# Supertile 3's norm moved behind up product 11 and turned by DMA, with one final tile on ScalarE and GpSimd

## The chip, the cores and the metric

One Trainium2 chip; the same program runs on 8 cores, each with its own tokens. The time is device microseconds of the slowest core, so it ends when the last of the eight is done. A core has a matmul engine (TensorE, PE in the rows, with PEld for its weight loads), VectorE (DVE), ScalarE (ACT), GpSimd (POOL), a queue for transfers issued by SyncE (SP), and 16 DMA engines that all queues share.

## The reference, cut to what matters

```python
def _layer(x, pool_hist, pos0, norm1_g, w_in, ...):
    h = _rmsnorm(x, norm1_g)
    z = h @ w_in                                   # [pool | u | v], 1536 columns
    a, u, v = z[..., :512], gelu(z[..., 512:1024]), gelu(z[..., 1024:])
    pool_out, new_hist = _pool_mixer(a, pool_hist, pos0, pool_w, pool_scale)
    gmlp_out = _gmlp_gate(u, v, gmlp_ws, gmlp_b)
    x = x + concatenate([pool_out, gmlp_out], axis=-1) @ w_out
    f = _rmsnorm(x, norm2_g) @ w_up                # 1024 -> 4096
    return x + square(relu(f)) @ w_down            # 4096 -> 1024
# one layer, then a final _rmsnorm(x, normf_g) is stored as y
```

## The kernel before

A core has 33 tiles of 128 tokens, in 11 **supertiles** of three tiles (384 tokens), numbered 0 to 10. The residual rows of supertile i stand in buffer `X[i % 3]`, three tiles of 512 KB each. Supertiles 0 and 1 share their MLP (the pair products, lines 667 and 687); from supertile 2 on the loop at line 963 does one at a time, and the front part of supertile i+1 (norm, input projection, mixers, output projection) is laid between the MLP products of supertile i.

The **MLP** of a supertile is 32 up products (`gen_UP`, PE line 705, eight matmuls each, then relu on ScalarE, line 709, and a square on VectorE, line 711), and eight groups of down products (`gen_DN`, line 764). The weights stream from the scratch tensor `scr` through a ring of five 1 MB slots, `RING`. When the last product that reads a slot has been issued, `ring_next` puts the load of the block five places on into SyncE's queue (line 650); it waits there for that product.

The **up products** use five PSUM banks in turn; product m uses bank (m+3) % 5, so product 0 needs bank 3, which the pair down products (line 687, added to X by VectorE at line 691) have used just before.

The **norm** of a supertile (`gen_N1_elem`) is three squares on ScalarE with a running sum (line 317), two small GpSimd instructions (lines 324, 330), and three multiplies on VectorE into the buffers `HB` (line 341). `gen_N1_T` then turns each tile for the input projection into `HT`: for supertiles 0 to 3 by eight transposes on PE (line 352) and a copy on ScalarE (line 356); from supertile 4 on by one DMA transpose from SyncE's queue for each tile (line 362). The input projection `gen_WI_au` (PE line 432) reads all three tiles of `HT`.

The **final norm** (`gen_final`) is three squares, two GpSimd instructions and three VectorE multiplies (line 802); the stores to `yall` are issued by SyncE for supertile 0 (`gen_ystore`, line 813) and by GpSimd for the others. The x loads (`gen_L`, line 268) go through GpSimd's queue, but those of supertile 3 go through SyncE's. A load of x into a buffer waits until the stores that read the buffer have landed.

The order of every engine's work is that of the `add` calls in the program; each engine runs its own list in order, and a wait holds all that stands behind it on the same engine. Around the change the order is: `gen_pair_DN(3, 0, 0)`, `(3, 1, 0)`, the final norm of supertile 0, `gen_pair_DN(3, 0, 1)`, a ring load, the stores of supertile 0, `gen_pair_DN(3, 1, 1)`, a ring load, the final norm of supertile 1 with its stores, the x loads of supertile 3, and then the loop for supertile 2 (line 970 on).

Of the kernel before, what the change touches and what calls it, by code (L numbers as in the profile page):

```python
# [8 lines left out]
AF = mybir.ActivationFunctionType  # L9
ALU = mybir.AluOpType  # L10
# [3 lines left out]
NT = 3  # L14
# [21 lines left out]
class Prog:  # L36
# [12 lines left out]
    def add(self, eng, fn, reads=(), writes=(), dma=None, after=()):  # L49
        waits = [self.lastw[k] for k in after]  # L50
        for r in reads:
            w = self.lastw.get(r)
            if w is not None:
                waits.append(w)
        for wr in writes:
            w = self.lastw.get(wr)
            if w is not None:
                waits.append(w)
            waits.extend(self.readers.get(wr, ()))
        ch = self.engchan[eng] if dma is None else self.chan(dma, 16)  # L60
        ch.count += ch.inc
        ev = Ev(ch, ch.count)
        for r in reads:
            self.readers.setdefault(r, []).append(ev)
        for wr in writes:
            self.lastw[wr] = ev
            self.readers[wr] = []
        self.ops[eng].append((fn, waits, ch))
        return ev
# [48 lines left out]
def build_nc():  # L118
# [28 lines left out]
    with contextlib.ExitStack() as es:  # L147
# [116 lines left out]
        def gen_L(i, q="pool"):  # L264
            b = i % NXB
            for n in range(NT):
                t = i * NT + n
                add(q, lambda e, b=b, n=n, t=t: e.dma_start(out=X[b][:, n, :], in_=xall[t * 128:(t + 1) * 128, :]),
                    writes=[("X", b, n)], dma=f"xld{b}_{n}{q}")
# [143 lines left out]

        def gen_N1_T(i, n0=0, n1=NT):
            for n in range(n0, n1):
                if i > 3:
                    norm_T_dma(hbs[("1", i)][n], HT, ("HT", n), 16 + n * 128, f"tr1_{n}")
                else:
                    B = bufs(i)
                    norm_T(hbs[("1", i)][n], B.HT, B.HTk[n], B.ho + n * 128)  # L420
# [232 lines left out]
        def ring_next(i, q):  # L653
            ring_load(ring_at[(i, q)] + NRING)
# [24 lines left out]
        def gen_pair_DN(b, hh, h):  # L679
            q = 8 + 4 * hh + b  # L680
            s = ring_slot(0, q)
            for n in range(NT):
                ub = next_up()

                def mm(e, n=n, s=s, ub=ub):
                    for kk in range(8):
                        i_ = e.matmul(bank(ub)[:, :], lhsT=ST[:, h * 8 + kk, n * 128:(n + 1) * 128], rhs=RING[s][:, kk, :],  # L687
                                      start=(kk == 0), stop=(kk == 7))
                    return i_
                add("pe", mm, reads=[("ST", h * 8 + kk) for kk in range(8)] + [("RING", s)], writes=[("BANK", ub)])  # L690
                add("dve", lambda e, n=n, ub=ub: e.tensor_tensor(  # L691
                    out=X[h][:, n, hh * 512:(hh + 1) * 512], in0=bank(ub)[:, :], in1=X[h][:, n, hh * 512:(hh + 1) * 512],
                    op=ALU.add),
                    writes=[("BANK", ub), ("X", h, n)])

        def gen_UP(i, m0, m1):
            H2all = [("H2T", n) for n in range(NT)]
            for m in range(m0, m1):
                q = m // 4
                s = ring_slot(i, q)  # L700
                ub = (m + 3) % 5

                def mm(e, m=m, s=s, ub=ub):
                    for k in range(8):
                        i_ = e.matmul(bank(ub)[:, 0:TOK], lhsT=RING[s][:, k, (m % 4) * 128:(m % 4 + 1) * 128],  # L705
                                      rhs=H2T[:, k, :], start=(k == 0), stop=(k == 7))
                    return i_
                add("pe", mm, reads=H2all + [("RING", s)], writes=[("BANK", ub)])
                add("act", lambda e, m=m, ub=ub: e.activation(out=ST[:, m, :], in_=bank(ub)[:, 0:TOK], func=AF.Relu),  # L709
                    writes=[("BANK", ub), ("ST", m)])  # L710
                add("dve", lambda e, m=m: e.tensor_tensor(out=ST[:, m, :], in0=ST[:, m, :], in1=ST[:, m, :], op=ALU.mult),  # L711
                    writes=[("ST", m)])
                if m % 4 == 3:
                    ring_next(i, q)
# [77 lines left out]
                    gen_tail(i, n, 1, 512 + p0, 512 + p1, ub, n + j, j == len(parts) - 1)  # L792
                gen_tail_out(i, n)

        def gen_final(i, tiles=None, squares_done=False, store=True):
            b = i % NXB
            tiles = list(range(NT)) if tiles is None else tiles
            srcs = [(X[b][:, n, :], [("X", b, n)]) for n in tiles]
            norm_stats("f", srcs, squares_done=squares_done)
            for j, n in enumerate(tiles):  # L800
                t = i * NT + n
                add("dve", lambda e, n=n, j=j: e.scalar_tensor_tensor(  # L802
                    out=X[b][:, n, :], in0=X[b][:, n, :], scalar=RS["f"][:, j:j + 1], in1=GFB[:],
                    op0=ALU.mult, op1=ALU.mult),
                    reads=[("RS", "f", j), "GFB"], writes=[("X", b, n)])
            if store:
                gen_ystore(i, tiles)

        def gen_ystore(i, tiles, q="pool"):
            b = i % NXB  # L810
            for n in tiles:
                t = i * NT + n
                fin_y[(q, b, n)] = add(q, lambda e, n=n, t=t: e.dma_start(out=yall[t * 128:(t + 1) * 128, :], in_=X[b][:, n, :]),
                                    reads=[("X", b, n)], dma=f"yst{b}_{n}{q}")
# [137 lines left out]
        gen_N2_T(2)  # L952
        gen_pair_DN(3, 0, 0)
        gen_pair_DN(3, 1, 0)
        gen_final(0, store=False)
        gen_pair_DN(3, 0, 1)
        ring_next(0, 11)
        gen_ystore(0, range(NT), "sp")
        gen_pair_DN(3, 1, 1)
        ring_next(0, 15)  # L960
        gen_final(1)
        gen_L(3, "sp")
        for i in range(2, NS):
            nxt = i + 1 < NS
            last = i == NS - 1
            gen_UP(i, 0, 4)
            if i > 2 and i + 2 < NS:
                gen_L(i + 2)
            if i == 2:
                gen_UP(i, 4, 17)  # L970
                gen_N1_elem(3)
                gen_L(4)
                gen_UP(i, 17, 22)
                for n in range(NT):
                    gen_N1_T(3, n, n + 1)
                    gen_UP(i, 22 + n, 23 + n)
                gen_WI_au(3)
                gen_WI_v(3)
                gen_PL(3)
                gen_UP(i, 25, 27)  # L980
                pieces = gen_PG_pieces(3)
                for k in range(4):
                    pieces[k]()
                    gen_UP(i, 27 + k, 28 + k)
                gen_UP(i, 31, 32)
                gen_WO_pe(3)
                gen_N2_elem(3)
                gen_DN(i, 0, 0)
                gen_DN(i, 0, 1)
                gen_DN(i, 0, 2)  # L990
                gen_N2_T(3)
            else:
                gen_UP(i, 4, 8)
                if nxt:
                    gen_WI_au(i + 1)
                    gen_WI_v(i + 1)
                    gen_PL(i + 1)
                gen_UP(i, 8, 18)
                pieces = gen_PG_pieces(i + 1) if nxt else []
                for k in range(8):  # L1000
                    if pieces and k % 2 == 0:
                        pieces[k // 2]()
                    gen_UP(i, 18 + k, 19 + k)
                gen_UP(i, 26, 30)
                if nxt:
                    gen_WO_pe(i + 1)
                    gen_N2_elem(i + 1)
                gen_UP(i, 30, 32)
                if last:
                    add("act", lambda e: e.activation(out=JUNK[:, 0:4], in_=RT[:], func=AF.Sqrt),  # L1010
                        reads=[("RT", n) for n in range(4)], writes=["JUNK"])
                gen_DN(i, 0, 0)
                gen_DN(i, 0, 1)
                gen_DN(i, 0, 2)
                if nxt:
                    gen_N2_T(i + 1)
            gen_DN(i, 0, 3, tile_final=last)
            if last:
                gen_DN_last(i)
                break  # L1020
            gen_DN(i, 1, 0)
            if i < NS - 2:
                gen_N1_elem(i + 2)
            gen_DN(i, 1, 1)
            gen_DN(i, 1, 2)
            if i + 2 < NS:
                gen_N1_T(i + 2)
            gen_DN(i, 1, 3)
            gen_final(i)
# [69 lines left out]
```

How the kernel before makes its waits and increments, by code:

```python
        def run(engname, e, final=False):  # L77
            waited = {}
            pe_ch = prog.engchan["pe"]
            for fn, waits, chn in prog.ops[engname]:
                need = {}
                for w in waits:
                    if engname == "pe" and w.chan is pe_ch:
                        continue
                    if w.val > need.get(w.chan, 0):
                        need[w.chan] = w.val
                for ch, v in need.items():
                    if waited.get(ch, 0) >= v:
                        continue
                    e.wait_ge(ch.sem, v)
                    waited[ch] = v
                ins = fn(e)
                ins.then_inc(chn.sem, chn.inc)
            if final:
                for ev in final_waits:
                    e.wait_ge(ev.chan.sem, ev.val)
```

## Time and profile before

| | us |
|---|---|
| median of 3 runs | 1247.89 (1247.71 to 1248.1) |
| the profiled execution | 1248.57 |
| span of its slowest core, core 4 | 1247.0 |
| spans of the other cores | 1242.1 to 1245.2 |
| PE busy on core 4 | 1232.1 (99%) |
| DVE, ACT, POOL busy on core 4 | 502.7, 374.6, 97.1 |

The profile is of one execution, on every core. A span is from the first to the last instruction of a core. The chain that ended last follows the last instruction back to what released it, and so on. In a row of a timeline the square bracket is the idle time of the engine before the group, and what ended it. "To landing" is the time from the issue of a transfer to the last of its semaphore updates.

### The profile page before, as it was taken

How to read it: one execution, taken by the hardware profiler on the slowest of the kernel's cores; microseconds unless marked ns; L12 is line 12 of the kernel's file. 1: busy time of each engine (PE TensorE's matmuls, PEld its weight loads, DVE VectorE, ACT ScalarE, POOL GpSimd, SP SyncE). 2: the span in 40 equal slices, each digit the busy share in tenths (PEclk: the TensorE clock that was granted, in tenths of full speed). 3: DMA queues.
4: the chain of work that ended last, by engine and by line, in shares of the span. 5: the costliest groups of instructions: out<-in, count | busy, mean ns of one | idle time of the engine just before them, and what ended most of it. 6: DMA issues, size and time to landing. Idle time of an engine off the chain costs nothing.

```text
span 1247.0 us, 19037 instructions; the slowest of 8 cores (1242.1 to 1247.0 us)
## 1 busy us (share of the span) xinstructions
PE 1232.1 (99%) x6777; PEld 651.3 (52%) x6777; DVE 502.7 (40%) x924; ACT 374.6 (30%) x722; POOL 97.1 (8%) x171
## 2 busy tenths in 40 slices
PE   8999999999999999999999999999999999999998
PEld 4455545545545554554555455455545545554554
DVE  5664434444533442543344254234415433450313
ACT  5353313125322330432233043223304322420422
POOL 5010000001010010100001010100101010000000
PEclk9999999999999999999999999999999999999999
DMA  8999967459449537745853874585378448547862
GB/s 175 176 221 222 242 161 199 112 142 322 157 131 257 203 127 227 240 169 157 257 195 130 225 253 169 152 248 195 135 227 260 169 143 244 156 145 228 253 203 85
DMA packets 90671, 240.48 MB, mean 193 GB/s; under 512 B 57665, under 2 KB 57729, under 8 KB 67794
## 3 DMA queue, kind: packets, MB, share of 16 engines
q1 hardware_dynamic: 78480, 189.74, 49.2%
q0 software_dynamic: 11920, 49.19, 17.0%
q8 instruction: 56, 0.92, 0.3%
q10 hardware_dynamic: 178, 0.33, 0.1%
q14 instruction: 37, 0.30, 0.1%
HBM read 214.40 MB, written 34.43 MB: 200 GB/s over the span
## 4 chain that ended last, share of the span: by engine, by line
PE 96%; DMA 2%; POOL 1%; DVE 0%; issue 0%; ACT 0%; SPq 0%; POOLq 0%; ACTq 0%; DVEq 0%
PE ps L705 30%; PE ps L764 28%; PE ps L589 9%; PE ps L432 8%; PE ps L667 7%; PE ps L687 7%; PE ps L457 5%; PE ps L786 2%; DMA WV<-w_v 1%; PE ps L537 1%; DMA X<-xall 1%; PE ps L352 1%; POOL RS L330 0%; POOL RS L324 0%; DVE HB L341 0%
## 5 line engine op out<-in xcount | busy, mean ns | idle before, releaser
L705 PE MATMUL ps<-H2T,RING 128*128 128x384 bf16 x2304 | 384.1, 327 | 0.5 <-DVE X L691 0.5
L764 PE MATMUL ps<-RING,ST 128*128 128x512 bf16 x1632 | 353.7, 380 | 0.0
L705 PEld LDWEIGHTS ps<-H2T,RING 128*128 128x128 bf16 x2304 | 223.8, 98 | 147.8 <-issue 0.9
L764 PEld LDWEIGHTS ps<-RING,ST 128*128 128x128 bf16 x1632 | 159.6, 98 | 191.8
L317 ACT ACTIVATE JUNK<-X 128x1024 bf16<-128x1024 f32 (+2 forms) x104 | 106.4, 1023 | 436.0 <-DVE X L771 290.1
L709 ACT ACTIVATE ST<-ps 128x384 bf16<-128x384 f32 x288 | 140.5, 489 | 208.5 <-PE ps L705 208.4
L711 DVE TENSOR_TENSOR ST<-ST 128x384 bf16<-128x384 bf16 x288 | 96.9, 357 | 193.7 <-ACT ST L709 193.4
L771 DVE TENSOR_TENSOR X<-ps,X 128x512 f32<-128x512 f32 x48 | 33.2, 692 | 222.3 <-PE ps L764 222.3
L432 PE MATMUL ps<-HT,WAU 128*128 128x384 bf16 (+1 forms) x640 | 106.7, 327 | 1.4 <-DMA WAU<-w_au 1.4
L432 PEld LDWEIGHTS ps<-HT,WAU 128*128 128x128 bf16 x640 | 62.3, 98 | 43.4 <-issue 2.4
L687 PE MATMUL ps<-RING,ST 128*128 128x512 bf16 x384 | 83.7, 379 | 0.1
L593 DVE TENSOR_TENSOR X<-ps,X 128x512 f32<-128x512 f32 x66 | 45.5, 691 | 57.9 <-PE ps L589 57.7
L672 ACT ACTIVATE ST<-ps 128x384 bf16<-128x384 f32 x64 | 31.4, 490 | 105.0 <-PE ps L667 101.1
L589 PE MATMUL ps<-WOUT,DT 128*128 128x512 bf16 x240 | 61.6, 380 | 0.0
L589 PE MATMUL ps<-WOUT,MIXT 128*128 128x512 bf16 x240 | 61.6, 379 | 0.0
L687 PEld LDWEIGHTS ps<-RING,ST 128*128 128x128 bf16 x384 | 37.3, 98 | 45.4 <-issue 0.8
L457 PE MATMUL ps<-WV,HT 128*128 128x512 bf16 x240 | 55.1, 388 | 2.5 <-DMA WV<-w_v 2.5
L691 DVE TENSOR_TENSOR X<-ps,X 128x512 f32<-128x512 f32 x48 | 32.5, 690 | 46.2 <-PE ps L687 46.2
L341 DVE SCALAR_TENSOR_TENSOR HB<-X,RS,G1B 128x1024 bf16<-128x1024 f32 x33 | 41.1, 1282 | 23.8 <-DMA H2T<-HB 11.7
L324 POOL TENSOR_SCALAR RS<-SS 128x3 f32<-128x3 f32 (+2 forms) x28 | 14.8, 527 | 460.6 <-ACT JUNK L317 460.3
L802 DVE SCALAR_TENSOR_TENSOR X<-X,RSf,GFB 128x1024 f32<-128x1024 f32 x30 | 36.8, 1282 | 31.2 <-POOL RSf L330 26.8
L341 DVE SCALAR_TENSOR_TENSOR HB<-X,RS,G2B 128x1024 bf16<-128x1024 f32 x30 | 36.8, 1281 | 23.2 <-POOL RS L330 23.2
(103 smaller groups left out, 732.9 us busy)
## 6 DMA issues: line engine op xcount, KB each, us to landing
RING<-scr SPq DMA_DIRECT2D x144, 1024.0 KB, 5.5
RING<-w_mlp POOLq DMA_DIRECT2D x16, 1024.0 KB, 16.6
scr<-RING SPq DMA_DIRECT2D x16, 1024.0 KB, 10.4
yall<-X POOLq DMA_DIRECT2D x27, 512.0 KB, 11.5
X<-xall POOLq DMA_DIRECT2D x24, 512.0 KB, 5.5
X<-xall SPq DMA_DIRECT2D x9, 512.0 KB, 7.7
yall<-X SPq DMA_DIRECT2D x5, 512.0 KB, 8.2
WOUT<-w_out POOLq DMA_DIRECT2D x2, 1024.0 KB, 26.7
```

What stands on the lines that cost most here:

```text
L317: add("act", lambda e, ap=ap, j=j: e.activation(out=JUNK[0:np_, 0:ap.shape[-1]], in_=ap, func=AF.Square, scale=1.0 / 32, accum_out=SS[kind ...
L341: add("dve", lambda e: e.scalar_tensor_tensor(out=HB[hb][:], in0=ap, scalar=RS[kind][:, j:j + 1], in1=gb[:], op0=ALU.mult, op1=ALU.mult), ...
L432: i_ = e.matmul(bank(fb)[:, h0:16 + TOK], lhsT=WAU[:, m, k, :], rhs=B.HT[:, k, ho - 16 + h0:ho + TOK], start=(k == 0), stop=(k == 7))
L457: i_ = e.matmul(bank(fb)[:, :], lhsT=B.HT[:, k, B.ho + n * 128:B.ho + (n + 1) * 128], rhs=WV[:, k, :], start=(k == 0), stop=(k == 7))
L589: i_ = e.matmul(bank(fb)[:, :], lhsT=src[:, n * 128:(n + 1) * 128], rhs=WOUT[:, hh, k, :], start=(k == 0), stop=(k == 7))
L593: add("dve", lambda e, n=n, hh=hh, fb=fb: e.tensor_tensor(out=X[b][:, n, hh * 512:(hh + 1) * 512], in0=bank(fb)[:, :], in1=X[b][:, n, hh * ...
L667: i_ = e.matmul(bank(ub)[:, 0:TOK], lhsT=RING[s][:, k, (m % 4) * 128:(m % 4 + 1) * 128], rhs=HX[:, k, :], start=(k == 0), stop=(k == 7))
L687: i_ = e.matmul(bank(ub)[:, :], lhsT=ST[:, h * 8 + kk, n * 128:(n + 1) * 128], rhs=RING[s][:, kk, :], start=(kk == 0), stop=(kk == 7))
L705: i_ = e.matmul(bank(ub)[:, 0:TOK], lhsT=RING[s][:, k, (m % 4) * 128:(m % 4 + 1) * 128], rhs=H2T[:, k, :], start=(k == 0), stop=(k == 7))
L709: add("act", lambda e, m=m, ub=ub: e.activation(out=ST[:, m, :], in_=bank(ub)[:, 0:TOK], func=AF.Relu), writes=[("BANK", ub), ("ST", m)])
L711: add("dve", lambda e, m=m: e.tensor_tensor(out=ST[:, m, :], in0=ST[:, m, :], in1=ST[:, m, :], op=ALU.mult), writes=[("ST", m)])
L764: i_ = e.matmul(bank(n)[:, :], lhsT=ST[:, kg * 8 + kk, n * 128:(n + 1) * 128], rhs=RING[s][:, kk, :], start=(kg == 0 and kk == 0), stop=(k ...
```

## The change

Three parts. The norm of supertile 3 and its turning move from behind up product 16 (and 21 to 24) of supertile 2 to behind up product 11; the turning goes by DMA from SyncE's queue instead of PE and ScalarE; the x loads of supertile 4, which stand behind the norm in GpSimd's queue, move along. The stores of supertile 0 and the x loads of supertile 3 each stand one ring load earlier in SyncE's queue. In the final norm of supertile 0, tile 2 is scaled by ScalarE and multiplied by the gain on GpSimd, in place of one VectorE instruction.

```diff
         def gen_N1_T(i, n0=0, n1=NT):
             for n in range(n0, n1):
-                if i > 3:
+                if i > 2:
                     norm_T_dma(hbs[("1", i)][n], HT, ("HT", n), 16 + n * 128, f"tr1_{n}")
...
-        def gen_final(i, tiles=None, squares_done=False, store=True):
+        def gen_final(i, tiles=None, squares_done=False, store=True, apart=()):
...
+                if n in apart:
+                    add("act", lambda e, n=n, j=j: e.activation(out=X[b][:, n, :], in_=X[b][:, n, :], func=AF.Copy,
+                                                                scale=RS["f"][:, j:j + 1]),
+                        reads=[("RS", "f", j)], writes=[("X", b, n)])
+                    add("pool", lambda e, n=n: e.tensor_tensor(out=X[b][:, n, :], in0=X[b][:, n, :], in1=GFB[:], op=ALU.mult),
+                        reads=["GFB"], writes=[("X", b, n)])
+                    continue
...
-        gen_final(0, store=False)
+        gen_final(0, store=False, apart=(2,))
+        gen_ystore(0, range(NT), "sp")
         gen_pair_DN(3, 0, 1)
         ring_next(0, 11)
-        gen_ystore(0, range(NT), "sp")
         gen_pair_DN(3, 1, 1)
+        gen_L(3, "sp")
         ring_next(0, 15)
         gen_final(1)
-        gen_L(3, "sp")
...
-                gen_UP(i, 4, 17)
+                gen_UP(i, 4, 12)
                 gen_N1_elem(3)
+                gen_N1_T(3)
                 gen_L(4)
-                gen_UP(i, 17, 22)
-                for n in range(NT):
-                    gen_N1_T(3, n, n + 1)
-                    gen_UP(i, 22 + n, 23 + n)
+                gen_UP(i, 12, 25)
                 gen_WI_au(3)
```

## Rows read from the trace of the kernel before

**Rows 1.** Page of core 4: busy time of the engines; chain that ended last.

```profile
PE 1232.1 (99%) x6777; PEld 651.3 (52%) x6777; DVE 502.7 (40%) x924; ACT 374.6 (30%) x722; POOL 97.1 (8%) x171
...
PE 96%; DMA 2%; POOL 1%; DVE 0%; issue 0%; ACT 0%; SPq 0%; POOLq 0%; ACTq 0%; DVEq 0%
```

**Rows 2.** Spans and granted clocks of the cores.

```profile
core 1: 1245.1 us, clock 0.999
...
core 4: 1247.0 us, clock 0.999
```

**Rows 3.** Chain that ended last, core 4, 270 to 315 us: start, duration, what.

```profile
277.28 1.29 DVE X L691 x2
...
278.71 26.18 PE ps L705 x160
...
308.11 0.61 PE ps L352 x8
...
310.02 0.45 PE ps L352 x8
...
313.51 1.59 PE ps L432 x9
```

**Rows 4.** Busy windows, core 1, 276 to 318 us: engines, PEclk, DMA share, GB/s.

```profile
276.00:318.00 42.00, 41.04 (x267) 24.64 (x266) 20.13 (x40) 23.45 (x44) 5.57 (x10) 1.00 0.99 314
```

**Rows 5.** Timeline of PE, core 1, 274 to 320 us: start, duration, instruction.

```profile
276.73 26.16 PE L705 MATMUL ps<-H2T,RING 128*128 128x384 bf16 x160 [0.48 <-DVE X L691]
303.23 2.76 PE L705 MATMUL ps<-H2T,RING 128*128 128x384 bf16 x16 [0.34 <-ACT JUNK L317]
...
311.49 8.77 PE L432 MATMUL ps<-HT,WAU 128*128 128x384 bf16 x53
```

**Rows 6.** Timeline of DVE, core 4, 225 to 345 us.

```profile
271.89 3.68 DVE L802 SCALAR_TENSOR_TENSOR X<-X,RSf,GFB 128x1024 f32<-128x1024 f32 x3 [3.16 <-POOL RSf L330]
275.49 3.67 DVE L691 TENSOR_TENSOR X<-ps,X 128x512 f32<-128x512 f32 x6
```

**Rows 7.** Groups by line: POOL of core 4, whole run; ACT line 743.

```profile
L249 POOL TENSOR_SCALAR_AFFINE_SELECT IDB<-IDB 128x128 bf16<-128x128 bf16 x1 | 0.3, 292 | 0.2 <-POOL IDB L248 0.2
...
L743 ACT ACTIVATE X<-X,RSf x3: 722/722/722, 1230.0 to 1243.4; 128x512 f32<-128x512 f32 x3
```

**Rows 8.** Core 4: SP timeline, DMA issues at 385 and 391.5 us, line 362.

```profile
385.69 0.32 SPq L650 DMA_DIRECT2D RING<-scr  x1
386.16 6.58 SPq L362 DMA_TRANSPOSE HT<-HB  x3
...
391.51 1.23 SPq L362 DMA_TRANSPOSE HT<-HB  x1
...
RING<-scr SPq DMA_DIRECT2D x1, 1024.0 KB, 5.8
...
HT<-HB SPq DMA_TRANSPOSE x1, 4.5
...
DMA to landing us min/median/max: 3.1/5.8/7.9
```

**Rows 9.** DMA issues of core 1, 285.5 to 286.2 us, then 292 to 293 us: to landing.

```profile
yall<-X POOLq DMA_DIRECT2D x1, 512.0 KB, 14.3
...
RING<-scr SPq DMA_DIRECT2D x1, 1024.0 KB, 16.6
```

**Rows 10.** Timeline of POOL, core 1, 270 to 320 us.

```profile
285.84 0.53 POOL L813 DMA_DIRECT2D yall<-X  x1 [0.65 <-DVE ST L711]
...
303.63 0.89 POOL L330 TENSOR_TENSOR RS<-RS,NEGH 128x3 f32<-128x3 f32 x1
304.49 1.68 POOL L268 DMA_DIRECT2D X<-xall  x3
```

**Rows 11.** DMA packets: core 1, 271 to 312 us; core 4, 273 to 310.9 us.

```profile
DMA packets 2256, 11.47 MB, mean 280 GB/s; under 512 B 238, under 2 KB 238, under 8 KB 1478
...
DMA packets 2236, 11.64 MB, mean 307 GB/s; under 512 B 240, under 2 KB 240, under 8 KB 1394
```

**Rows 12.** DMA by queue, core 4, 312 to 316 us: packets, MB, share.

```profile
q0 software_dynamic: 243, 0.91, 74.5%
q1 hardware_dynamic: 45, 0.24, 24.0%
```

**Rows 13.** PE timelines 40 to 53 us of cores 4, 1; core 4's busy windows.

```profile
44.94 7.03 PE L457 MATMUL ps<-WV,HT 128*128 128x512 bf16 x24 [2.51 <-DMA WV<-w_v]
...
44.43 5.34 PE L457 MATMUL ps<-WV,HT 128*128 128x512 bf16 x24 [1.73 <-DMA WV<-w_v]
...
45.00:50.00 5.00, 5.00 (x16) 1.90 (x17) 1.65 (x6) 0.60 (x1) 1.78 (x3) 0.66 1.02 170
```

## The prediction

> **What bounds the kernel now.** I read the page first: PE is busy for 99% of the slowest core's span, and 96% of the chain that ended last lies on it [rows 1]. So a microsecond counts only where PE stands still or does work that the change removes, and almost all that the change touches on other engines is worth nothing by itself. Then the spans: core 4 sets the time at 1247.0 us, but core 1 is only 1.9 us behind, at 1245.1 [rows 2], so a wait that hits core 1 harder than core 4 can make core 1 the last. The chain around the change [rows 3] shows what there is to win. PE waits for two VectorE evictions before up product 0 starts at 278.71, then 20 up products run in 26.18 us (1.31 each), then come two more, the first transposes at 308.11, and the input projection of supertile 3 at 313.51. Last I read the DMA, because the change turns a PE step into transfers: on core 1, from 276 to 318 us, the engines' share is 0.99 at 314 GB/s [rows 4]. The DMA is as full there as PE is. A transfer that is moved there does not run beside others, it runs behind or between them.
>
> **Part 1, PE loses the transposes.** On core 4, 22 products of 1.30 us end at 278.71 + 28.6 = 307.31. The three products between the transposes take 3.90. The projection starts at 313.51, so 313.51 - 307.31 - 3.90 = 2.30 us are transposes (0.61 for the first group, 0.45 for one later) and the wait ahead of them [rows 3]. Without them the projection could start 32.5 us (25 products) behind product 0. ScalarE also loses three copies, which cost the path nothing.
>
> **Part 2, the wait of product 0.** PE stands 0.48 us before product 0, on core 1 too [rows 5]. On VectorE the three final multiplies start at 271.89 and the six evictions behind them at 275.49 [rows 6]. With two multiplies the evictions begin 1.2 us sooner; the one that product 0 needs is then no longer late, and next to come is the last pair product itself. I take 0.48 us. The new GpSimd multiply has no row of its kind. From below: the VectorE one takes 1.28 us (3.68 for three, overlapped). From above: GpSimd's select of 128 columns took 0.29 us [rows 7], an estimate of 2.3 us for 1024 columns if all of it scales. ScalarE's scaling of 512 columns took 0.72 us [rows 7], so about 1.1 for 1024, in time in which ScalarE has nothing to do. Tile 2 would then be stored from about 275 or 276 us on, as before (its store was issued as the third, behind 271.89 + 3.68 = 275.57). Nobody but that store and what stands behind it waits for GpSimd.
> The page "SBUF — State Buffer" of the Trainium skill (section "Who interferes with whom") says that a VectorE instruction with two SBUF inputs and a GpSimd one that reads SBUF do not run together, and the second to issue waits for the whole of the first. No row here has such a pair of that length. It speaks against this part; what it would do is rival 3.
>
> **Part 3, SyncE's queue.** The stores of supertile 0 go ahead of one ring load, the x loads of supertile 3 ahead of another. The ring load that is now behind the x loads is needed by up product 16, 20.8 us behind product 0; all of it is the same bytes in another order, and I cost it at nothing. Its cover is thin on core 1, where PE already waited 0.34 us before product 20 at 303.23 [rows 5], hidden until now by the wait for the transposes; up to 1 us more if that cover goes. The bounds are 0 and 1.
>
> **Part 4, the turning by DMA.** This is where I expect the result. The norm is five products earlier (6.5 us, plus the 0.48), so `HB` is ready about 22 us behind product 0, and SyncE can issue the three transposes from there. The projection wants them landed at 32.5. How long they take: in a later supertile a ring load was issued at 385.69 and landed 5.8 us later, at 391.5. The three transposes were issued from 386.16, but the third not until 391.51, that is when the ring load had landed, and it landed 4.5 us after that; the shortest of all 48 took 3.1 [rows 8]. So transposes don't overtake ring loads: SyncE's queue is served in order, and the last of three lands 3.1 to 4.5 us behind the ring load ahead; I take the middle, 3.8. In the new place the load ahead is the one of up product 11's ring slot. On core 1 it was issued 15.8 us behind product 0, at 292.57, and took 16.6 us [rows 9], so it landed at 309.2. That alone gives 309.2 + 3.8 = 313.0, which is later than the 308.75 at which PE would want it (276.25 + 32.5).
> Then the x loads of supertile 4. They stand behind the norm in GpSimd's queue, were issued at 304.49 [rows 10], and now go about 7 us sooner, at 297.5, the third when the last store of supertile 1 has landed (285.84 + 14.3 = 300.1) [rows 9, 10]. So all 1.57 MB of them get in front of or between the transposes. That GpSimd's transfers take their share from SyncE's is seen on core 4 from 312 to 316 us, when they ran beside ring loads: 0.91 MB against 0.24 [rows 12].
> So I count bytes. Ahead of the last transposes there are five ring loads (5.24 MB), the stores of supertiles 0 and 1 and the x loads of 3 and 4 (6.29 MB), 11.53 MB in all. Before the change core 1 had moved 11.47 MB by 312.0 us, core 4 11.64 by 310.9 [rows 11]. With the engines full, order does not change that: core 1 is there at 312.2, core 4 at 310.6. Plus 3.8: `HT` is ready at 316.0 on core 1 and 314.4 on core 4. Before, the projection started at 311.49 [rows 5] and 313.51 [rows 3]. Core 1 loses 4.5 us, core 4 loses 0.9. Parts 1 and 2 are swallowed by this wait, since it ends with a transfer and not with PE.
> **The clock.** PE then stands idle on core 1 for 316.0 - 308.75 = 7.2 us. On core 4, behind an idle time of 2.51 us, the granted clock was 0.66 over 45 to 50 us, and 24 matmuls took 7.03 us; on core 1, behind 1.73 us, the same 24 took 5.34 [rows 13]. A wait of 7.2, or of 4.3 on core 4, should bring the same: 7.03 - 5.34 = 1.7 us more. Bounds 0 and 1.7; I take 1.7.
>
> **Sum, in the profiled execution.** Core 1: 1245.1 + 4.5 + 1.7 = 1251.3. Core 4: 1247.0 + 0.9 + 1.7 = 1249.6. Core 1 becomes the last, 4.3 us above 1247.0, so 1248.57 becomes 1252.9. The median of the runs was 0.68 below that execution: **1252.2**. All else behind the projection is PE work as before, and the ring loads held up in SyncE's queue by the transposes are for down products some 30 us later.
>
> **The rivals.**
> 1. *The x loads of supertile 4 take nothing from the transposes* (they start too late, or the queues don't share as on core 4). Then core 1 has `HT` at 313.0, 1.5 us later than before, and with the clock 1248.3; core 4 about in time. The time is +1.3 us, 1249.2, no change that can be measured. For it: GpSimd's transfers start moving some time after their issue. Against it: the full DMA.
> 2. *The transposes are in time*, so that parts 1 and 2 come whole: 2.30 + 0.48 = 2.8 us on every core, 1245.1. It needs the transposes landed within 10 us of their issue. For it: the landing times of 3.1 to 7.9 us of all others [rows 8]. Against it: none of those was issued behind a DMA backlog of 16 us [rows 9]. This is the other side; it decides at a landing 32.5 us behind product 0.
> 3. *The GpSimd multiply holds VectorE.* If it starts as tile 0's multiply ends, tile 1's waits some 2 us, the evictions start at about 276.4 instead of 275.49, and product 0 starts 0.9 later than before instead of 0.48 earlier: 1.4 us lost. Together with transposes in time it gives 1246.5. Together with my forecast it is swallowed. The Trainium skill's page "SBUF — State Buffer" (same section) would have it so if GpSimd issues first.
> 4. *Worse than the forecast*: ring load late for product 16 on top, or the transposes thinned by GpSimd's packets beyond the 3.8: up to 1255.
>
> **Chances.** Forecast 0.60; rival 1, 0.20; rival 2, 0.10; rival 3 with the transposes in time, 0.04; rival 4, 0.06. A measurement of this kernel can tell about 0.2%, or 2.5 us, from no change. Slower: 0.60 + 0.06 = 0.66; within: 0.20 + 0.04 = 0.24; faster: 0.10 (its 2.8 us is just over). The range holds the forecast with its bounds (without the clock's part 1250.5; with the transposes at 4.5 and 1 us more for a late ring load 1253.9) and reaches down over rivals 1 and 3: 1246.0 to 1254.5. It leaves out rival 2 and most of rival 4.
>
> **What would show it.** In the profile of after: no idle time before up product 0 (part 2; if VectorE's second final multiply begins 2 us late, rival 3); the projection's first matmul waiting for the DMA HT<-HB, by about 7 us on core 1 and 4 on core 4 (part 4), the third transpose issued when the ring load ahead lands; the x loads of supertile 4 landed before it; PE's granted clock below 1.00 in the 5 us behind the wait; core 1 the last. The prediction is wrong if the transposes are served ahead of the ring loads, or if the backlog is gone by 300 us.

## The result, and the profile after

| | before | after |
|---|---|---|
| median of the runs, us | 1247.8 | 1272.7 (1259.6 to 1287.2) |
| undisturbed runs, us | 1247.4 to 1248.1 | 1259.62 and 1260.72 |
| profiled execution, its slowest core, us | 1248.57, core 4: 1247.0 | 1259.62, core 7: 1258.0 |

In half of the runs of the changed kernel the cores of one or both dies ran at a lower clock throughout; all that follows compares undisturbed runs. Their ratio is 1.0099 (95% interval 1.0075 to 1.0124). It is slower, as forecast, but by 12 us, outside the range.

The page of the changed kernel: first line, busy times, the chain, and the group of the input projection (columns as in section 5 of the page).

```profile
span 1258.0 us, 18995 instructions; the slowest of 8 cores (1253.9 to 1258.0 us)
...
PE 1232.1 (98%) x6753; PEld 651.1 (52%) x6753; DVE 503.3 (40%) x923; ACT 373.6 (30%) x720; POOL 97.7 (8%) x172
...
PE 93%; DMA 4%; SPq 1%; issue 1%; DVE 1%; POOL 1%; ACT 0%; DVEq 0%; ACTq 0%; POOLq 0%
...
L432 PE MATMUL ps<-HT,WAU 128*128 128x384 bf16 (+1 forms) x640 | 108.8, 331 | 15.2 <-DMA HT<-HB 14.0
```

PE is busy for 1232.1 us, as before [rows 1]: it has 24 transposes fewer, but its projection takes 2.2 us longer. Core 7's span is 11 us longer than core 4's was, and PE now has one idle time of 14.0 us, in front of the projection, ended by the DMA `HT<-HB`. The spans of three cores:

```profile
core 1: 1254.6 us, clock 0.995
...
core 4: 1254.0 us, clock 0.996
...
core 7: 1258.0 us, clock 0.993
```

Core 4 grew by 7.0, core 1 by 9.5, core 7 by 15.5 us (it had 1242.5). PE on core 4, then on core 7 (start, duration, group, idle time before it):

```profile
276.03 1.89 PE L687 MATMUL ps<-RING,ST 128*128 128x512 bf16 x8 [0.71 <-DVE X L691]
278.42 32.66 PE L705 MATMUL ps<-H2T,RING 128*128 128x384 bf16 x200 [0.50 <-DVE X L691]
318.74 12.33 PE L432 MATMUL ps<-HT,WAU 128*128 128x384 bf16 x64 [7.66 <-DMA HT<-HB]
```

```profile
275.56 32.66 PE L705 MATMUL ps<-H2T,RING 128*128 128x384 bf16 x200 [0.50 <-DVE X L691]
322.25 12.73 PE L432 MATMUL ps<-HT,WAU 128*128 128x384 bf16 x64 [14.04 <-DMA HT<-HB]
```

These answer [rows 3, 5]. From product 0 to the projection it was 34.8 us on every core; now 40.3 on core 4 and 46.7 on core 7, where the 25 products alone take 32.5. The 64 matmuls of the projection took 10.56 us before on every core, and take 12.33 and 12.73 now. Behind them all is as it was: from the end of the projection to the last matmul it takes 917.4 us, on all eight cores of both kernels.

VectorE and GpSimd around product 0, core 4:

```profile
270.71 4.58 DVE L809 SCALAR_TENSOR_TENSOR X<-X,RSf,GFB 128x1024 f32<-128x1024 f32 x2 [3.16 <-POOL RSf L330]
275.21 3.66 DVE L691 TENSOR_TENSOR X<-ps,X 128x512 f32<-128x512 f32 x6
```

```profile
271.84 2.37 POOL L806 TENSOR_TENSOR X<-X,GFB 128x1024 f32<-128x1024 f32 x1 [1.44 <-ACT X L803]
```

Three VectorE multiplies took 3.68 us before [rows 6]. Two take 4.58 now: the second starts at 271.91 and takes 3.37 us instead of 1.28, and GpSimd's multiply (2.37 us) had started 0.07 us before it. That this is the cause is shown by e8 below.

Core 7 while the transposes were in flight (columns as in [rows 4]: the last three are the granted clock, the DMA engines' share and GB/s), and two of the transfers that GpSimd's and SyncE's queues had in hand between 302 and 304 us, the third x tile (issued at 303.0) and the second transpose (its issue ran from 300.1 to 307.8):

```profile
298.00:303.00 5.00, 5.00 (x32) 3.01 (x31) 4.85 (x11) 1.88 (x4) 0.53 (x1) 1.00 1.02 282
303.00:308.00 5.00, 5.00 (x33) 2.93 (x30) 1.44 (x4) 1.97 (x4) 0.53 (x1) 1.00 1.13 190
308.00:313.00 5.00, 0.22 (x2) 0.00 (x0) 0.36 (x1) 0.49 (x1) 0.00 (x0) 1.00 1.41 74
313.00:318.00 5.00, 0.00 (x0) 0.00 (x0) 0.00 (x0) 0.00 (x0) 0.00 (x0) 0.50 1.31 89
```

```profile
X<-xall POOLq DMA_DIRECT2D x1, 512.0 KB, 18.1
HT<-HB SPq DMA_TRANSPOSE x1, 21.3
```

Between 308 and 318 us the DMA engines are busy (the share is over 1 because packets overlap) and move 74 to 89 GB/s, a quarter of the 314 of [rows 4]; over 307.5 to 320 us the mean is 82. The x tile took 18.1 us to land, the transpose 21.3. The packet records show the same. A transpose moves in packets of 256 bytes. On core 7, from 30 to 45 us behind product 0, they took 18 ns at the median but 103 on average; with the x loads held back (e1 below, core 4, 300 to 312 us) the two figures are 18 and 29. The long ones come in groups of mostly 4 to 15 that start within some 50 ns and take about 170 or 330 ns each, with 4096-byte packets of the x loads among them (159 ns at the median in e1). The records don't tell which packets share an engine.

From the landing of the ring load ahead of the transposes to that of the last transpose, the forecast had 3.8 us. It is 17.6 on core 7 (28.9 to 46.6 us behind product 0), 13.0 to 14.9 on cores 0, 2 and 5, where that ring load also landed early (27.8 to 29.6), and 7.7 to 8.4 on cores 1, 3, 4 and 6, where it landed at 31.4 to 32.5.

### The profile page after: what moved, and what is told of

It reads as the page before. It is cut to its first block, busy times and chain, and to the rows that moved or that the text cites. A ratio compares the mean times of both kernels' runs of the same rounds, so it can differ in the third digit from the quotient of the medians.

```text
span 1258.0 us, 18995 instructions; the slowest of 8 cores (1253.9 to 1258.0 us)
## 1 busy us (share of the span) xinstructions
PE 1232.1 (98%) x6753; PEld 651.1 (52%) x6753; DVE 503.3 (40%) x923; ACT 373.6 (30%) x720; POOL 97.7 (8%) x172
## 3 DMA queue, kind: packets, MB, share of 16 engines
q0 software_dynamic: 11920, 49.19, 17.6%
## 4 chain that ended last, share of the span: by engine, by line
PE 93%; DMA 4%; SPq 1%; issue 1%; DVE 1%; POOL 1%; ACT 0%; DVEq 0%; ACTq 0%; POOLq 0%
PE ps L705 29%; PE ps L764 28%; PE ps L589 9%; PE ps L432 8%; PE ps L667 7%; PE ps L687 6%; PE ps L457 4%; DMA WOUT<-w_out 2%; PE ps L786 2%; DMA HT<-HB 1%; SPq L362 1%; DMA X<-xall 1%; PE ps L537 1%; PE ps L352 0%; POOL RS L330 0%
## 5 line engine op out<-in xcount | busy, mean ns | idle before, releaser
L705 PE MATMUL ps<-H2T,RING 128*128 128x384 bf16 x2304 | 383.6, 326 | 0.5 <-DVE X L691 0.5
L672 ACT ACTIVATE ST<-ps 128x384 bf16<-128x384 f32 x64 | 31.4, 491 | 104.9 <-PE ps L667 100.8
L691 DVE TENSOR_TENSOR X<-ps,X 128x512 f32<-128x512 f32 x48 | 32.5, 689 | 46.2 <-PE ps L687 46.2
L667 PE MATMUL ps<-H2T,RING 128*128 128x384 bf16 x256 | 46.2, 326 | 0.0
L341 DVE SCALAR_TENSOR_TENSOR HB<-X,RS,G2B 128x1024 bf16<-128x1024 f32 x30 | 36.8, 1281 | 23.3 <-POOL RS L330 23.3
## 6 DMA issues: line engine op xcount, KB each, us to landing
scr<-RING SPq DMA_DIRECT2D x16, 1024.0 KB, 10.4
```

What stands on the lines that cost most here:

```text
L341: add("dve", lambda e: e.scalar_tensor_tensor(out=HB[hb][:], in0=ap, scalar=RS[kind][:, j:j + 1], in1=gb[:], op0=ALU.mult, op1=ALU.mult), ...
```

## The experiments

Where a figure below is given for all cores, it is read from each core's timeline, as shown for one.

### Are the x loads the cause? e1, e2, e6, e3

**e1_x_gated**: the x loads of supertile 4 wait for the last transpose.

```diff
-                gen_L(4)
+                gen_L(4, gate=[("HT", 2)])
```

> The changed kernel, with the x loads of supertile 4 held until the last DMA transpose of supertile 3 has landed. Theory A (transposes and GpSimd's x loads in flight together slow each other far below the rate of either): the last transpose lands some 4 us behind the ring load ahead of it, PE waits about 3 us before the projection on core 4 (7.66 in the changed kernel) and under 2 on core 7 (14.04), no core loses more than about 5 us, and the time is near 1251. Theory B (transposes are slow in this stretch by themselves, behind the ring loads and with both cores of a pair loading): the waits stay at 7 to 14 us and the time near 1260.

```profile
311.60 10.56 PE L432 MATMUL ps<-HT,WAU 128*128 128x384 bf16 x64 [0.71 <-DMA HT<-HB]
```

```profile
305.00:310.00 5.00, 5.00 (x33) 3.02 (x31) 1.60 (x5) 1.78 (x4) 0.00 (x0) 1.00 1.18 247
...
306.50:311.50 5.00, 4.39 (x28) 2.44 (x25) 1.31 (x4) 1.96 (x4) 0.00 (x0) 1.00 1.08 162
```

```profile
DMA to landing us min/median/max: 3.1/6.0/8.4
```

The wait before the projection falls from 7.66 to 0.71 us on core 4, from 14.04 to nothing on core 7, and is at most 1.15 on any core; the projection is back at 10.56 us. The longest landing of a transpose on the slowest core is 8.4 us, and from the ring load ahead to the last transpose it is 2.9 to 4.8 us on the eight cores. The DMA engines move 247 GB/s in the first window above, which still has part of the ring load in it, and 162 in the second: with transposes alone the rate falls too. Of all stretches of 5 us with a DMA share of 0.95 or more, the lowest on each core moves 142 to 162 GB/s here. In the changed kernel it moves 58 to 86 on cores 0, 2, 5 and 7, and 119 to 167, about as with transposes alone, on the other four. Ratio to the kernel before 1.0007 (0.9997 to 1.0016). So nearly the whole loss needs GpSimd's x loads in flight beside the transposes (theory A). I had expected 3 us of wait to stay on core 4; the ring load ahead landed 30.3 us behind product 0 there, against 31.8 in the changed kernel, and the last transpose 2.9 us behind it.

**e2_x_one_gated**: only the third x tile waits.

```diff
-                gen_L(4)
+                gen_L(4, n1=2)
+                gen_L(4, gate=[("HT", 2)], n0=2)
```

> The changed kernel, with only the third x load of supertile 4 held until the last transpose has landed; the other two go as in the changed kernel. Theory A: the two loads land before or early in the transposes on cores 0, 2, 5, 7, where the wait before the projection falls from 9 to 14 us to under 5; on the others it falls to about 5. Theory B: waits as in the changed kernel. A plain count of bytes (theory C, my forecast's) would give 0.5 MB less ahead of the transposes, so 1.6 us less wait on every core.

```profile
316.96 13.23 PE L432 MATMUL ps<-HT,WAU 128*128 128x384 bf16 x64 [6.44 <-DMA HT<-HB]
```

The waits are 3.6 to 6.4 us, where they were 6.6 to 14.0 with all three and 0 to 1.2 with none. The first two tiles (1.05 MB, 3.3 us at 314 GB/s) cost 3 to 6 us, the third (0.52 MB, 1.7 us) up to 8 more. The count of bytes (theory C) fails: it gave 1.6 us less than the changed kernel, and the mean wait of the eight cores fell by 4.6, from 9.3 to 4.7. Theory A had the fall right, but cores 0 and 7 stayed slightly above its 5 us (5.3 and 5.9). The time of its one run is 1254.79.

**e6_x_on_sp**: the same loads, from SyncE's queue behind the transposes, with no gate.

```diff
-                gen_L(4)
+                gen_L(4, "sp")
```

> The changed kernel, with the x loads of supertile 4 issued from SyncE's queue, behind the transposes, instead of GpSimd's; nothing is held by a semaphore. Theory A (two queues with transposes in one of them disturb each other; within one queue they go in order): the last transpose lands by 34 us behind up product 0 on every core, as with the loads held back, and the wait before the projection is under 1.5 us. If any transfer issued near the transposes disturbs them, whatever its queue, the waits are 4 us or more.

```profile
313.10 10.56 PE L432 MATMUL ps<-HT,WAU 128*128 128x384 bf16 x64 [1.91 <-DMA HT<-HB]
```

The waits are 0 to 1.9 us on the eight cores (1.91 is core 4), the projection takes 10.56 everywhere, and the last transpose lands 2.9 to 4.8 us behind the ring load ahead, as in e1; the one run took 1248.4. That is slightly over the 1.5 expected and far from the 4 of the other theory: in one queue the loads go behind the transposes and leave them alone. But SyncE came to the first x load only when it had issued the third transpose, 28.8 to 31.5 us behind product 0, where GpSimd issues it at 21.3. So this run doesn't tell whether it is the other queue or the earlier start that does the harm.

**e3_pe_turn**: everything of the change but the turning by DMA.

```diff
-                if i > 2:
+                if i > 3:
                     norm_T_dma(hbs[("1", i)][n], HT, ("HT", n), 16 + n * 128, f"tr1_{n}")
...
-                gen_UP(i, 12, 25)
+                gen_UP(i, 12, 22)
+                for n in range(NT):
+                    gen_N1_T(3, n, n + 1)
+                    gen_UP(i, 22 + n, 23 + n)
```

> The changed kernel, but supertile 3 is turned by PE between up products 22 and 24, as before the change; its norm stays behind up product 11, and the queue order and the split final norm stay too. If all of the loss comes from the transposes by DMA, the projection waits for nothing, the wait for HB (0.64 us) is gone, and the time is within 1 us of the kernel before: about 1247.9, with 0.7 us lost to the split final norm. If the new queue order costs by itself (ring load late for product 16, x late for the norm), PE waits inside the up products and the time is over 1249.

```profile
277.73 28.76 PE L705 MATMUL ps<-H2T,RING 128*128 128x384 bf16 x176 [0.51 <-DVE X L691]
306.32 0.61 PE L352 MATMUL ps<-IDB,HB 128*128 128x128 bf16 x8
...
311.69 8.61 PE L432 MATMUL ps<-HT,WAU 128*128 128x384 bf16 x52
```

The x loads of supertile 4 are as early as in the changed kernel, and nothing waits: from product 0 to the projection it takes 33.96 us, 0.80 less than before, with no gap in the up products on any core. Ratio 0.9998 (0.9988 to 1.0008). The x loads do harm only beside transposes by DMA, and the new queue order (part 3) costs nothing.

### The split final norm: e4, e8

**e4_apart_only** is the kernel before with `apart=(2,)`, **e8_gps_behind_dve** the same with one wait more:

```diff
                     add("pool", lambda e, n=n: e.tensor_tensor(out=X[b][:, n, :], in0=X[b][:, n, :], in1=GFB[:], op=ALU.mult),
-                        reads=["GFB"], writes=[("X", b, n)])
+                        reads=["GFB"], writes=[("X", b, n)], after=[("X", b, 1)])
```

> The kernel before, with the split final norm of supertile 0 alone (tile 2 scaled on ScalarE, multiplied on GpSimd). If GpSimd's multiply holds VectorE's second final multiply (rival 3 of the prediction), the two VectorE multiplies take 4.6 us instead of 2.5 and PE stands about 1.2 us around up product 0 instead of 0.48: 0.7 us slower, about 1248.6. If not, the wait of 0.48 us is gone: about 1247.4.

> The kernel before with the split final norm alone, and GpSimd's multiply held until VectorE's second final multiply is done. If the two held each other at the same time, VectorE's two multiplies take 2.5 us again (4.6 with the split alone), and the wait before up product 0 is gone: PE stands under 0.3 us there. If ScalarE's in-place scaling is what slowed VectorE, they still take over 4 us.

PE of core 4 in e4, and then in e8:

```profile
275.82 1.89 PE L687 MATMUL ps<-RING,ST 128*128 128x512 bf16 x8 [0.72 <-DVE X L691]
278.21 6.99 PE L705 MATMUL ps<-H2T,RING 128*128 128x384 bf16 x42 [0.51 <-DVE X L691]
```

```profile
261.81 18.29 PE L687 MATMUL ps<-RING,ST 128*128 128x512 bf16 x84
279.94 5.36 PE L705 MATMUL ps<-H2T,RING 128*128 128x384 bf16 x32
```

VectorE and GpSimd in e8:

```profile
273.77 2.48 DVE L809 SCALAR_TENSOR_TENSOR X<-X,RSf,GFB 128x1024 f32<-128x1024 f32 x2 [3.16 <-POOL RSf L330]
```

```profile
276.52 2.36 POOL L806 TENSOR_TENSOR X<-X,GFB 128x1024 f32<-128x1024 f32 x1 [3.06 <-DVE X L809]
```

In e4 PE stands 0.72 before the last pair product and 0.51 before product 0, 1.22 us in all (0.48 before), on every core, and VectorE's two multiplies take 4.58. In e8 GpSimd starts when they are done; they take 2.48, and all idle time is gone. ScalarE's scaling is in both, so it is not the cause: GpSimd's multiply holds VectorE's, which also has two inputs from SBUF. GpSimd's own takes 2.36 us in both. That is rival 3 of the prediction. The Trainium skill ("SBUF — State Buffer", section "Who interferes with whom") has it that two such instructions share a port pair as an exclusive lock, and that the order of issue decides who is blocked. The trace agrees: on core 4 of e4 GpSimd's starts at 271.62 and ends at 273.98, VectorE's second starts at 271.69 and ends at 275.07, 1.1 us behind it. The other order of issue occurs in no run here. Both times (1248.38 and 1250.04, one run each) lie within what the start of the program varies, so the verdict rests on the gaps.

### What makes the slowing: e7, e10, e12, e13, e14

All but e14 are built on e1, and move x loads beside the second norm's transposes (`H2T<-HB`), about 85 us behind product 0, where there is no backlog; e14 is the changed kernel with its loads in another order. Of each edit only the calls that issue the loads are shown.

```python
 e7    gen_L(4, gate=[("HB", hbs[("2", 3)][0])])       # behind DN(2, 0, 2)
 e10   gen_L(4, gate=[("BANK", 2)])                    # behind DN(2, 0, 2)
 e12   gen_L(4, gate=[("BANK", 2)], n0=2)              # one tile, the others as in e1
 e13   gen_L(4, gate=[("BANK", 0)], n0=2)              # the same tile, behind DN(2, 0, 3)
 e14   gen_L(4, n0=2); gen_L(4, n1=2)                  # behind gen_N1_T(3), no gate
```

> The kernel with the held x loads, but they are issued from GpSimd's queue when the first tile of supertile 3's second norm is ready, so that they run beside the three transposes H2T<-HB, at a place where the DMA engines have no backlog (the ring takes 1 MB in 5.2 us there). Theory A: these three transposes, which land 3 to 8 us behind their issue in all kernels so far, take over 12 us. If a backlog in the ring queue is needed for the slowing (theory B), they land within 9 us.

It settles nothing: the x loads were issued 9 to 10 us ahead of the transposes, and on every core they had landed before the ring load ahead of the transposes had.

> As e7_mix_elsewhere, but the x loads of supertile 4 are issued when the third down group of supertile 2 is done, which is also when SyncE issues the ring load and the three transposes behind it, so that the loads' data really move beside the transposes. With the loads elsewhere the third transpose landed 11 us behind the issue of the first. A count of bytes (1.57 MB at 320 GB/s) would make that 16 us at most. Theory A (the two kinds slow each other beyond their bytes): over 18 us on some cores, and a stretch in which the engines are busy and move under 150 GB/s. Theory B (it takes the ring's backlog too): 16 us or less, and no such stretch.

> The kernel with the held x loads, but the third x tile of supertile 4 is issued at the end of the third down group, beside the later transposes H2T<-HB; the first two are issued as in e1. Three tiles there made the last transpose land some 4 to 5 us later, what their 1.57 MB take. By bytes one tile costs 1.6 us. If a thin stream of x packets is worse than a deep one for transposes that go in step, one tile costs as much as three or more: over 3 us on some cores.

> As e12, with the third x tile issued some 3 us later, when the transposes are already queued, as in the changed kernel. By bytes 1.6 us or less; by the theory of the steps over 3 us on some cores. If neither this nor e12 costs more than its bytes, the slowing belongs to the place.

Landing times of all transposes on the slowest core, in e10, e12 and e13 (before 3.1/5.8/7.9 [rows 8], e1 8.4 at most):

```profile
DMA to landing us min/median/max: 3.1/5.9/11.9
```

```profile
DMA to landing us min/median/max: 3.1/6.1/9.1
```

```profile
DMA to landing us min/median/max: 3.0/6.3/12.3
```

From the issue of the first to the landing of the third of these transposes, mean of the eight cores (range): e1 10.9 us (10.3 to 11.5); e10, three tiles, 14.6 (13.5 to 16.1), which is 3.7 for 1.57 MB, less than their bytes (5.0 at 314 GB/s); e12, one tile issued with the transposes, 11.7 (11.0 to 12.4), 0.8 for 0.52 MB; e13, the same tile 2.5 us later, 13.2 (11.8 to 14.4), 2.3 and on two cores over 3. So theory A in the strong form of e10 (over 18 us) falls. Its other sign, a stretch under 150 GB/s, is no test, since transposes with no x load beside them have such stretches too (the lowest 5 us of each core in e1 at this place: 111 to 174). But core 7 of e10, whose transposes took longest, went far below that:

```profile
371.50:376.50 5.00, 5.00 (x25) 2.29 (x24) 0.00 (x0) 3.45 (x6) 0.22 (x1) 1.00 1.41 81
```

So the slowing is not bound to the new place. And one late tile costs nearly three times as much as one that is early, and more than its bytes. The late issue counts, as far as one profiled execution of each shows.

> The changed kernel, with its three x loads of supertile 4 issued in the order 2, 0, 1, so that all wait for the last store of supertile 1 and start together some 27 us behind up product 0, behind the issue of the first transpose. By the theory of the steps a deep queue costs about its bytes: the transposes land 4 to 6 us later than with the loads held (33 us), near 38, on all cores, and no core has the 44 to 47 us of the changed kernel. If the place or the late issue makes the slowing, it is as bad as in the changed kernel or worse, with three tiles in it: over 44 us on several cores.

```profile
326.82 12.82 PE L432 MATMUL ps<-HT,WAU 128*128 128x384 bf16 x64 [12.56 <-DMA HT<-HB]
```

```profile
310.00:315.00 5.00, 4.25 (x27) 2.35 (x24) 1.24 (x5) 1.96 (x4) 0.00 (x0) 1.00 1.19 84
315.00:320.00 5.00, 0.00 (x0) 0.00 (x0) 0.30 (x1) 0.00 (x0) 0.00 (x0) 0.78 1.28 78
```

On core 0 the last transpose landed 45.1 us behind product 0, with a stretch of 78 to 84 GB/s like core 7's above; cores 2, 3, 5, 6 and 7 have 37.0 to 40.5; cores 1 and 4, whose three transposes had all been issued when the loads began, 34.7 and 32.6. The mean of the eight is 38.2, where the changed kernel has 41.9 and my theory of the steps (a thin stream of x packets is worse for transposes than a deep one) gave 38. But it gave it for every core, and none at 44 or more: a deep queue of x packets does not protect the transposes, and the theory, as I had put it, is wrong. What the runs show is that x loads from the other queue which start while transposes are under way can cut the rate of both to a quarter, by an amount that differs between cores with the same program. Why the delay reaches nearly 13 us on one core at the new place (17.6 against 4.8 in e1) and stays under 5 at the later one is open.

### The change once more, and a version from the findings

> The changed kernel once more, unaltered, to size its loss on more executions. If the wait before the projection is the loss, each core again waits 6 to 14 us there, the projection takes 12.3 to 13.5 us instead of 10.6, all behind it takes 917.4 us as in every kernel with the old order, and the ratio to the kernel before is near 1.010.

Its one run that can be compared took 1260.93, beside 1247.27 to 1247.54 for the kernel before: 1.011. In its profile cores 2 and 3 have a mean granted clock of 0.995, as in the first: they waited 11.0 and 10.4 us, and the projection took 12.6 and 13.0. The size of the loss is what it was.

**e9_all_hidden** keeps what worked: the norm behind product 11, the turning by DMA, e1's gate; the final norm is not split, its multiplies stand between evictions, and the projection gets two more products of cover. So that these fit, the first down group moves ahead of the output projection, and the turning of the second norm behind the fourth down group (that part of the edit is not shown).

```diff
-        gen_final(0, store=False, apart=(2,))
-        gen_ystore(0, range(NT), "sp")
-        gen_pair_DN(3, 0, 1)
+        norm_stats("f", [(X[0][:, n, :], [("X", 0, n)]) for n in range(NT)])
+        gen_pair_DN(3, 0, 1, (0, 1, None))      # final multiply of tile 0, 1 behind eviction 0, 1
+        gen_ystore(0, (0, 1), "sp")
         ring_next(0, 11)
-        gen_pair_DN(3, 1, 1)
-        gen_L(3, "sp")
+        gen_pair_DN(3, 1, 1, (None, 2, None))
+        gen_ystore(0, (2,), "sp")
+        gen_L(3, "sp", n1=2)
         ring_next(0, 15)
+        gen_L(3, "sp", n0=2)
...
-                gen_L(4)
-                gen_UP(i, 12, 25)
+                gen_L(4, gate=[("HT", 2)])
+                gen_UP(i, 12, 27)
                 gen_WI_au(3)
...
+                gen_DN(i, 0, 0)
                 gen_WO_pe(3)
```

> A version made from the findings: supertile 3 turned by DMA behind up product 11, the x loads of supertile 4 held until the last transpose has landed, the projection behind up product 26 instead of 24, the output projection of supertile 3 behind the first down group, and the final norm of supertile 0 not split: its three VectorE multiplies stand between the evictions, so that product 0's bank comes free in time. If all waits are as read, PE stands nowhere between the last pair product and the first down product: 2.3 + 0.5 = 2.8 us less than before, 0.998 of its time. If a new wait comes up in the later order, 0.5 to 2 us of that are lost.

```profile
core 2: 1244.4 us, clock 0.997
```

```profile
261.83 16.35 PE L687 MATMUL ps<-RING,ST 128*128 128x512 bf16 x75
278.02 35.26 PE L707 MATMUL ps<-H2T,RING 128*128 128x384 bf16 x216
313.12 10.56 PE L432 MATMUL ps<-HT,WAU 128*128 128x384 bf16 x64
```

From the pair products to the down products PE has no idle time before any group on seven cores, and 0.1 us in all on core 7; the slowest core takes 1244.4. Against the kernel before 0.9974 (0.9964 to 0.9984): about 3.2 us, where 2.8 was expected. It beats both kernels. The idle times are gone as planned; how much of the gain each part brings was not measured apart.

## Why the prediction was wrong

- **Part 1** was right in size: without the transposes and their wait the projection could start 32.5 us behind product 0, and does so on cores 3 and 7 of e1. The gain is there in e9.
- **Part 2, wrong.** I took 0.48 us gained; it was 0.73 lost (1.22 us of idle time for 0.48). The failing step is "the evictions begin 1.2 us sooner" (they began 4.5 us behind the first final multiply, where it had been 3.6): I put rival 3 at 0.04 with the transposes in time, though the rows gave a start for GpSimd's multiply (when ScalarE is done with tile 2, as tile 0's multiply ends) at which it had to meet tile 1's. I named 1.4 us lost against my forecast; it was 1.2. The GpSimd multiply took 2.37 us, by bounds of 1.28 and 2.3.
- **Part 3** was right: nothing waits for the new order (e3).
- **Part 4, the mechanism was right, the size not.** The projection waits for `HT<-HB`, the transposes go behind the ring loads, and the x loads of supertile 4 are in their way. Two terms failed. The first is "with the engines full, order does not change that": the count of bytes took the rate as given, and on core 7 it was 82 GB/s over 12.5 us. The second is the 3.8 us from the ring load ahead to the last transpose: with the x loads beside them the transposes took 7.7 to 17.6, and 2.9 to 4.8 without. `HT` was to be ready on core 4 36.2 us behind product 0, and was ready at 40.2; on core 7, for which I made no sum, it was 46.6.
- **Core 1 came out nearly right by luck.** There it was 39.8 forecast and 40.5 measured. But without the x loads I had 36.8 (rival 1), and e1 has 32.6: in my row of the ring load ahead, two more ring loads were in flight (issued 21.0 and 26.2 us behind product 0), which now stand behind the transposes in the same queue. That they made the difference is likely, not shown. The x loads, which I had at 3.0 us, cost 7.9. One error hid the other.
- **Which core is last.** I summed cores 1 and 4 only, since they were the slowest before. Core 7 had 4.5 us to spare and lost 15.5: 1.4 up to product 0 (0.7 of them part 2, the rest the start of the program, which moves product 0 between 273 and 282 us over the cores and runs), 11.9 from there to the projection, 2.2 in it. With a loss that differs by core, each core needs its own sum.
- **The clock** was right in kind and short in size: 1.7 us forecast, 1.8 on core 4, 2.2 on core 7, and 1.8 to 2.9 on the eight cores, with no order by the length of the wait (2.9 is core 6, with the shortest, 6.6 us). On core 7 the granted clock was 0.50, the lower of its two levels (1.2 GHz), from 313 to 318 us, and PE had stood still since 308.2. In all runs the projection took 10.56 us behind waits up to 1.96 us and from 12.2 up behind those of 3.5 and more; between (2.1 to 3.0) both occur.
- **The rivals.** Rival 1 (x loads take nothing) fell: e1 shows that they took nearly all. Rival 2 fell in the changed kernel, and came true in e9. Rival 3's mechanism came true, and its 0.7 us lost lay ahead of the wait. Rival 4 (the transposes thinned by GpSimd's packets beyond 3.8 us) is what happened; I gave it 0.06 and an end at 1255. The range ended 5 us short because its upper bound was made of landing times of transposes that had no traffic from the other queue beside them.

## What to carry to other kernels

When a PE transpose is turned into a DMA transpose, look not only at what its own queue holds, but at what another queue may start while it runs, and put that transfer behind it (the same queue, or a wait for it); here that alone was worth nearly 12 us (e1 against the changed kernel). A bound on a wait must come from rows in which the same neighbours were present, and each core must be summed, not only the ones that were last. Work moved from VectorE to GpSimd was no relief here while both read two inputs from SBUF; placing the multiplies between evictions was.

## What the runs showed of the hardware

- DMA transposes and plain loads from another queue, started before or while they run, can move together at 82 GB/s over 12.5 us at a full DMA share (core 7 of the changed kernel; 314 in [rows 4]). Transposes without such loads had 142 to 162 in their lowest 5 us (e1). With the loads held back, or in the same queue behind them, the last transpose landed 2.9 to 4.8 us behind the ring load ahead; with them beside, 7.7 to 17.6. How far it goes is not the same on two cores, and its cause is open.
- A GpSimd multiply of 128x1024 f32 takes 2.37 us, and a VectorE multiply of two SBUF inputs that starts 0.07 us behind it stretches from 1.28 to 3.37 us (4.58 for the two instead of 2.48).
